# Input projection of the token mixer: float32 products become three single-pass products of split operands

## The reference, cut to what matters

```python
def token_mix(hx, hc, w_in, ...):
    def project(h):
        return jnp.split(h @ w_in, split_at, axis=-1)
    cq, cff, cfb, ci, cg, caq, cak, cav, cga, cgb = project(hc)
    ...
    xq, xff, xfb, xi, xg, xaq, xak, xav, xga, xgb = project(hx)
    xo, _, _ = hgrn_bidir(heads(xq, HG_HEADS), ..., cs_f, cs_b)
    ...
    y_x = merge(xo, xg, attend_blocks(xqa, keys, vals), xga, xgb)
...
x = x + g1 * y_x
x = x + g2 * expert_choice_moe(...)       # 16 experts, 12 MB of weights each
```

## Time and profile before

| | us |
|---|---|
| median of 3 runs | 1872.17 (1870.63 to 1873.43) |
| the profiled execution | 1873.85 |
| its span | 1872.1 |
| TensorE busy | 1716.0 (92%) |
| VectorE busy | 795.9 (43%) |
| ScalarE busy | 634.2 (34%) |
| GpSimd busy | 8.7 |
| first row of the projection to the end of its step 17 | 1083.6 to 1275.2 |
| expert stage | 1440 to 1872, 427 GB/s of loads |

### The profile page before, as it was taken

One profiled execution on the slowest core, in us unless ns is written; L12 is line 12 of the kernel. 1 busy time (PEld: TensorE's weight loads), 2 busy tenths in 40 slices (PEclk: granted clock), 3 DMA queues, 4 the chain that ended last, 5 costly groups with the idle time before them and its releaser, 6 DMA issues.

```text
span 1872.1 us, 30497 instructions
## 1 busy us (share of the span) xinstructions
PE 1716.0 (92%) x13205; PEld 1417.3 (76%) x13205; DVE 795.9 (43%) x1155; ACT 634.2 (34%) x899; POOL 8.7 (0%) x8
## 2 busy tenths in 40 slices
PE   8999999999999999999999999999999876765765
PEld 7999987899999999778999955877787442422422
DVE  6555697865566555224655522732512100000001
ACT  5444556644454444123444422415602010000101
POOL 0000010000000000000000000000000000000000
PEclk9999999999999999999999999999999997978987
DMA  9755456355545554552655532324566999999997
GB/s 291 241 166 193 158 181 201 118 198 181 183 154 188 192 180 140 164 173 94 199 182 192 164 113 68 113 90 158 216 258 247 427 425 427 427 426 426 426 427 327
DMA packets 189675, 427.45 MB, mean 228 GB/s; under 512 B 8004, under 2 KB 146678, under 8 KB 174485
## 3 DMA queue, kind: packets, MB, share of 16 engines
q1 hardware_dynamic: 189588, 426.19, 62.6%
HBM read 425.12 MB, written 1.05 MB: 228 GB/s over the span
## 4 chain that ended last, share of the span: by engine, by line
PE 74%; DMA 20%; DVE 3%; ACT 2%; issue 0%; another core or an unknown queue 0%; SPq 0%; DVEq 0%; ACTq 0%
PE banks L658 15%; PE banks L660 14%; PE banks L659 14%; DMA arena<-in_w_exp_down 5%; PE banks L1027 5%; PE banks L1003 3%; DMA ring<-in_w_exp_gate 3%; DMA xn<-in_w_exp_up 3%; DMA h<-in_w_exp_down 3%; DMA squares<-in_w_exp_gate 3%; DMA arena<-in_w_exp_up 2%; DMA ring<-in_w_exp_up 2%; PE banks L829 2%; PE banks L1300 1%; PE banks L781 1%; PE banks L1170 1%
## 5 line engine op out<-in xcount | busy, mean ns | idle before, releaser
L658 PE MATMUL banks<-x_split,w_split 128*128 128x256 f32 x1600 | 457.1, 286 | 9.5 <-DVE w_split L1873 4.0
L659 PE MATMUL banks<-x_split,w_split 128*128 128x256 f32 x1600 | 453.4, 283 | 0.0
L660 PE MATMUL banks<-x_split,w_split 128*128 128x256 f32 x1600 | 453.3, 283 | 0.0
L1873 DVE TENSOR_TENSOR w_split<-ring,w_split 128x1024 fp32r<-128x1024 f32 x288 | 346.5, 1224 | 237.7 <-ACT w_split L1396 237.3
L1396 ACT ACTIVATE w_split<-ring 128x1024 fp32r<-128x1024 f32 x287 | 295.2, 1051 | 190.5 <-PE banks L660 188.2
L658 PEld LDWEIGHTS banks<-x_split,w_split 128*128 128x128 f32 x1600 | 307.8, 192 | 13.3 <-issue 5.8
L659 PEld LDWEIGHTS banks<-x_split,w_split 128*128 128x128 f32 x1600 | 307.7, 192 | 0.3
L660 PEld LDWEIGHTS banks<-x_split,w_split 128*128 128x128 f32 x1600 | 307.7, 192 | 0.0
L658 PE MATMUL banks<-hid_split,w_split 128*128 128x256 f32 x704 | 199.6, 284 | 0.0
L659 PE MATMUL banks<-hid_split,w_split 128*128 128x256 f32 x704 | 199.2, 283 | 0.0
L660 PE MATMUL banks<-hid_split,w_split 128*128 128x256 f32 x704 | 199.2, 283 | 0.0
(11 more groups left out here) (387 smaller groups left out, 1945.8 us busy)
## 6 DMA issues: line engine op xcount, KB each, us to landing
ring<-in_ffn_w SPq DMA_DIRECT2D x131, 1024.0 KB, 5.3
arena<-in_w_exp_gate SPq DMA_DIRECT2D x13, 2048.0 KB, 45.9
ring<-in_w_mod SPq DMA_DIRECT2D x24, 1024.0 KB, 5.2
arena<-in_w_exp_down SPq DMA_DIRECT2D x12, 2048.0 KB, 45.0
arena<-in_w_exp_up SPq DMA_DIRECT2D x11, 2048.0 KB, 46.4
ring<-in_w_in SPq DMA_DIRECT2D x21, 1024.0 KB, 5.3
ring<-in_w_exp_down SPq DMA_DIRECT2D x9, 2048.0 KB, 44.3
ring<-in_w_exp_gate SPq DMA_DIRECT2D x7, 2048.0 KB, 45.9
```

The source lines that it names most:

```text
L658: mm(out_, hi, moving(0), start=start, stop=False, **kw)
L659: mm(out_, hi, moving(1), start=False, stop=False, **kw)
L660: return mm(out_, lo, moving(0), start=False, stop=stop, **kw)
L1873: ins = dve.tensor_tensor(half_part(n, o, 1), half_slot(n, o, columns), half_part(n, o, 0).bitcast(F32), ALU.subtract)
```

## The change

Steps 1 to 21 of the projection become three products of split operands, and step 0 stays as it is. ACT rounds the rows to `x_hi` (in ring slots 4 and 5) and DVE subtracts in place (`x_rest` is `xn`). For each piece ACT rounds both halves (`split_in`) into one of two buffers, the memory of the gates ga and gb (`w_gates`); the low part is the piece itself, subtracted in place in its ring slot (`w_rest`). DVE does both halves, except for pieces 8 to 15, whose second half GpSimd does. `split_in(s)` waits until the piece that had its buffer before has been multiplied, mostly s - 2, and the ring has only four slots from `mod_final` on. `ak` is multiplied once for both heads, and ACT writes the doubled halves with four copies; `av` is multiplied with the weights standing and then turned by four transposes. The last 1 MB loads of the mixer and the first expert tiles stand in another order. In `mla_a` the two halves of the last piece alternate for each k.

```diff
+FOUR_FROM = FIRST["mod_final"]
+PLACE = [n % SLOTS if n < FOUR_FROM else (n - FOUR_FROM) % 4 for n in range(FIRST["experts"])]
+PRIOR = [max([m for m in range(n) if PLACE[m] == PLACE[n]], default=None) for n in range(len(PLACE))]
+LOADS = [PLACE[:n + 1].count(PLACE[n]) for n in range(len(PLACE))]
+LAST_IN = [max(n for n in range(len(PLACE)) if PLACE[n] == p) for p in range(4)]
...
+        x_hi = nc.alloc_sbuf_tensor_at("x_hi", [P, KD, 2 * T], F32R, offset=ring_at + 4 * 4 * SLOT)
+        x_rest = nc.alloc_sbuf_tensor_at("x_rest", [P, KD, 2 * T], F32R, offset=xn_at)
+        w_rest = nc.alloc_sbuf_tensor_at("w_rest", [P, 4, KD, 256], F32R, offset=ring_at)
+        w_gates = split_tensor("w_gates", [P, 2, SLOT], gates_at)
+        w_roots = nc.alloc_sbuf_tensor_at("w_roots", [P, KD, P], F32R, offset=roots_at)
...
+        HI_BEFORE = {14: 12, 15: 12, 16: 14, 17: 15, 18: 16, 19: 17, 20: 18}
+        ON_POOL = list(range(8, 16))
+        LO_DVE = {(s, o): i + 1 for i, (s, o) in
+                  enumerate((s, o) for s in range(1, 21) for o in range(2) if o == 0 or s not in ON_POOL)}
...
+            branch_load(0)
             sp.wait_ge(sem("hg_normed"), 1)
             for i in (20, 8):
                 tile_load(i)
+            branch_load(1)
             sp.wait_ge(sem("att_ready"), 1)
             for i in (0, 1, 2, 3, 5):
                 tile_load(i)
-            w_out_load(2)
-            sp.wait_ge(slot_free, FIRST["branch"] + 1)
+            branch_load(2)
+            branch_load(3)
+            for i in (12, 13):
+                tile_load(i)
+            w_out_load(0)
             for i in (4, 6, 7):
                 tile_load(i)
+            w_out_load(1)
+            tile_load(9)
+            w_out_load(2)
             w_out_load(3)
-            sp.wait_ge(slot_free, FIRST["branch"] + 2)
-            tile_load(9)
-            for i in (17, 10):
-                wait_free(sp, N_EXPERTS + FIRST_IN_RING[i])
-                tile_load(i)
             sp.wait_ge(sem("merged_ready"), 2)
             for i in (14, 15):
                 tile_load(i)
-            for i in (11, 12, 13, 16):
-                wait_free(sp, N_EXPERTS + FIRST_IN_RING[i])
-                tile_load(i)
+            for p in sorted(range(4), key=lambda p: LAST_IN[p]):
+                sp.wait_ge(slot_free, LAST_IN[p] + 1)
+                tile_load((16, 17, 10, 11)[p])
...
-                for o in range(2):
-                    for k in range(KD):
-                        if j == 0 and o == 0 and k % 2 == 0:
-                            pe.wait_ge(sem("piece_normed"), NORM_PIECES["mla"] + k // 2 + 1)
-                        if j < 3:
+                if j < 3:
+                    for o in range(2):
+                        for k in range(KD):
+                            if j == 0 and o == 0 and k % 2 == 0:
+                                pe.wait_ge(sem("piece_normed"), NORM_PIECES["mla"] + k // 2 + 1)
                             last = mm(ps[:, j, o * T:o * T + T], slot(n)[:, k * 256 + o * P:k * 256 + o * P + P],
                                       x_in[:, k, :], start=(k == 0), stop=(k == KD - 1))
-                        else:
+                else:
+                    for k in range(KD):
+                        for o in range(2):
                             last = mm(ps[64 * o:64 * o + 64, j, 0:T], slot(n)[:, k * ROPE:k * ROPE + ROPE],
                                       x_in[:, k, :], start=(k == 0), stop=(k == KD - 1))
...
+                wait_rest(s, 0)
+                if name == "i":
+                    wait_rest(s, 1)
+                    lo = w_rest[:, PLACE[n], :, :]
+                    for t in range(4):
+                        for k in range(KD):
+                            tokens = slice(t * P, t * P + P)
+                            for part, (x_, w_) in enumerate(((x_hi, w_hi(s)), (x_hi, lo), (x_rest, w_hi(s)))):
+                                last = mm(ps[:, b + t // 2, (t % 2) * T:(t % 2) * T + T], x_[:, k, tokens], w_[:, k, :],
+                                          start=(k == 0 and part == 0), stop=(k == KD - 1 and part == 2))
+                    done(last)
+                    return
+                wide = name in ("ff", "fb", "ak", "av")
+                pe.wait_ge(sem("x_parts"), 6 if wide else 2 if step == 1 else 4)
+                rows = slice(0, 2 * T) if wide else slice(T, 2 * T)
+                for o in {"ak": (0,), "av": (1,)}.get(name, (0, 1)):
+                    if o == 1:
+                        wait_rest(s, 1)
+                    out_ = ps[:, b + (o if name in ("ff", "fb") else 0), :] if wide else ps[:, b, o * T:o * T + T]
+                    for k in range(KD):
+                        if step == 1 and o == 0 and k == 4:
+                            pe.wait_ge(sem("x_parts"), 4)
+                        hi, lo = w_hi_half(s, o)[:, k, :], w_lo_half(s, o)[:, k, :]
+                        mm(out_, hi, x_hi[:, k, rows], start=(k == 0), stop=False)
+                        mm(out_, hi, x_rest[:, k, rows], start=False, stop=False)
+                        last = mm(out_, lo, x_hi[:, k, rows], start=False, stop=(k == KD - 1))
...
+            for t in range(4):
+                last = pe.transpose(ps[:, 7, t * P:t * P + P], att_v[:, t, :], ident)
+            last.then_inc(sem("pe_mark"), 1)
...
+            def split_in(s):
+
+                n = w_in_slot(s)
+                if s >= 3:
+                    act.wait_ge(slot_free, w_in_slot(HI_BEFORE.get(s, s - 2)) + 1)
+                wait_full(act, n)
+                for o in range(2):
+                    fn(w_hi_half(s, o), w_in_half(s, o), ACT.Copy).then_inc(sem("w_hi_ready"), 1)
...
+            NEXT = {step: step + 2 for step in range(1, 12)} | {13: 14, 14: 15, 15: 16, 16: 17}
             for step in range(EARLY):
                 taken(step)
+                if step in NEXT:
+                    split_in(NEXT[step])
...
+            for s in ON_POOL:
+                pool.wait_ge(sem("w_hi_ready"), 2 * s)
+                pool.tensor_tensor(w_lo_half(s, 1), w_in_half(s, 1), w_hi_half(s, 1).bitcast(F32), ALU.subtract
+                                   ).then_inc(sem("w_rest_pool"), 1)
...
+            def rest_in(s):
+
+                for o in range(2):
+                    if (s, o) in LO_DVE:
+                        dve.wait_ge(sem("w_hi_ready"), 2 * s - 1 + o)
+                        dve.tensor_tensor(w_lo_half(s, o), w_in_half(s, o), w_hi_half(s, o).bitcast(F32), ALU.subtract
+                                          ).then_inc(sem("w_rest_ready"), 1)
...
+            REST = {0: 8, 1: 9, 2: 10, 3: 11, 4: 12, 5: 13, 7: 14, 8: 15}
             for r_ in range(ROUNDS):
+                if r_ in REST:
+                    rest_in(REST[r_])
```

More of the change, by code:

```diff
@@ L393, in wait_free @@
         def wait_free(sp, n, more=0):
-            if n >= SLOTS:
-                sp.wait_ge(slot_free, n - SLOTS + 1 + more)
+            if PRIOR[n] is not None:
+                sp.wait_ge(slot_free, PRIOR[n] + 1 + more)
         def wait_full(pe, n, more=0):
-            pe.wait_ge(slot_full[n % SLOTS], 16 * (n // SLOTS + 1) + more)
+            pe.wait_ge(slot_full[PLACE[n]], 16 * LOADS[n] + more)
         def wait_done(eng, n, more=0):
@@ L411, in slot @@
         def slot(n):
-            return ring[:, n % SLOTS, :]
+            return ring[:, PLACE[n], :]
         def half_slot(n, o, columns):
@@ L572, in _, with branch_load @@
                     mod_chunk(11)
[L573 to L576, removed]
+            def branch_load(j):
+                cols(FIRST["branch"] + j, (w_branch_a_2, w_branch_b_2)[j // 2][0], 512 * (j % 2), 512, 4)
             exp_tiles = [w[0].rearrange("e (j p k) c -> j e p (k c)", p=P, k=4)[j]
@@ L996, in project @@
                 b = 2 * (step % PAIRS) if step < EARLY else LATER_BANK[step - EARLY]
-                wait_full(pe, n)
                 if PAIRS <= step < EARLY:
                     pe.wait_ge(sem("proj_taken"), step - PAIRS + 1)
-                if name in ("ff", "fb"):
+                if step == 0:
+                    wait_full(pe, n)
                     for o in range(2):
                         for k in range(KD):
[L1003 to L1019, removed]
-                            last = mm(ps[:, b, t * P:t * P + P], xn[:, k, t * P:t * P + P],
-                                      slot(n)[:, k * 256 + P:k * 256 + 256], start=(k == 0), stop=(k == KD - 1))
-                else:
-                    for o in range(2):
-                        for k in range(KD):
-                            if step == 0 and o == 0 and k % 2 == 0:
+                            if o == 0 and k % 2 == 0:
                                 pe.wait_ge(sem("modulated"), SHIFTED["tokens"] + k // 2 + 1)
@@ L1036, in _ @@
                 if step == 0:
+                    pe.wait_ge(sem("mod_taken"), 4)
+                if step == 2:
                     pe.wait_ge(sem("squares_added"), 5)
@@ L1554, in _ @@
```

(27 more changed lines are left out.)

92 lines of the change are left out of this document (67 added, 25 removed).

## The result

The changed kernel takes 1846.4 us (median; 1845.5 to 1847.3) where the kernel before takes 1872.2: a ratio of 0.986, 95% interval 0.985 to 0.988, 25.8 us less. The forecast was 1842.6 with a range of 1830 to 1856.

What follows compares the result with a forecast made beforehand. TensorE was taken to bound the projection and DMA the expert stage. Gains of 38.1 + 2.3 - 0.7 + 2.7 = 42.4 us, less 12.8 lost in the rounds, left 29.6 off 1872.17: 1842.6 us, range 1830 to 1856.

Steps and rivals of the forecast that it cites:

- Bound and place of the gain: Before the experts: TensorE time gained ahead of 1435 moves the expert stream forward, except just ahead of two ACT/DVE places.
- The products: Projection up to the end of step 17: split products, 0.12 us narrow and 0.22 wide, save 38.1 us.
- near the record of the same width: Price of a split product of 512 columns, absent from the trace: taken as 0.22 us, bounds 0.215 and 0.240.
- The rounds: From step 8: DVE and GpSimd block each other on a shared port; 12.8 us lost, including 1 at the entry.
- the wait at the entry: When step 8 begins, DVE has no lead after the scans; 1 us of wait was counted.
- the branch of 14.8: In the rounds, DVE waits for GpSimd's port: 13.8 us plus 1 at the entry, weighted 0.75.
- The four transposes: Turning av behind step 17: 8 added records of 0.11 us, 0.9 less 0.2 idle, cost 0.7 us.
- Step 20: Between rotation and router: attention work waits only for it; steps 20 and 21 together gain 2.3 us.
- a clock under 1.0 in the projection: Granted TensorE clock in the projection: named as a sign against the whole forecast, with no size given.
- 18 and 19 give nothing: Steps ahead of waits for DVE's products ending at 1283.5 and 1316.0: shortening them gains nothing.
- mla_a: Half-array piece of the latent projection: alternating halves cut 6.3 us to 3.6, a gain of 2.7.
- The tail rivals: Slower GpSimd operations (3.5 us: 1849) or late expert tiles (four more: 1852); chance 0.17 together for 1847 to 1857.

Runs made afterwards that it cites:

- pool_left_out: The changed kernel without GpSimd's eight subtractions, TensorE taking the first half's low part for the second in pieces 8 to 15: 1835.98 us.
- warm: The changed kernel with eleven products of zeros in TensorE's idle time ahead of the attention's rotation (line 1162): 1844.70 us.
- pool_none: The changed kernel with VectorE making both halves of all low parts and GpSimd none: 1839.98 us, ratio 0.982.
- none_warm: The changed kernel with all low parts made by VectorE and eleven products of zeros ahead of line 1162: 1838.10 us, ratio 0.982.
- halves_alone: The kernel before with only the loop order of the latent projection's last matrix changed, so the halves alternate: 1870.04 us, ratio 0.9986.

## Why the prediction was right, and where its steps were off

**Bound and place of the gain: right.** TensorE's gain ahead of the experts reached the end: from the router on, both kernels take the same time to within 1.8 us, 1.15 of them step 21. SP's first reload of a buffer comes at 1407.2, and at 1435.4 before: 28.2 us earlier, nearly the whole of what the span lost.

**The products: one term too cheap.** Narrow steps took 5.74 to 5.84 us (forecast 5.76), steps 6 and 7 together 22.83 (23.04). The wide product was the open price, bounded by 0.215 and 0.240 and taken at 0.22; it measures 0.231 in steps 2 to 5 and 0.235 in ak and av. The step that failed is the choice "near the record of the same width". Half of that record is 0.215, and the split product lies 16 to 20 ns above it, where the one of 256 columns lies 12 ns above its half. So the extra grows with the columns, though less than in proportion; even the 12 ns once would have given 0.227, above the 0.22 that was taken. It cost 4 x 0.54 + 0.7 = 2.9 us.

**The rounds: the mechanism right, the sum right, its parts not.** From the end of step 7 (1160.4) to the last round's scores (1239.2) TensorE needed 78.8 us. Without any wait it is 65.2: 5.74 for step 8, and 59.4 for the eight distances as `pool_left_out` has them. So 13.6 were lost, where the sum had 12.8, weighted from 14.8 (VectorE always waits) and 6.7 (GpSimd does). All eight meetings went the first way. But the wait at the entry was 4.1 us and not 1: `pool_left_out` shows 2.0 of it as DVE's own list, and the rest is GpSimd's first operation, which fell on a scan, ahead of the rounds. Step 8 then ran 2.65 us longer, at a clock of 0.50 for part of it, and the sum had nothing for that. Against it, four distances were long by 0.6, 2.1, 2.1 and 2.0 us, 6.8 in all, where the sum had 13.8 for six rounds. The fifth distance was 7.4 us: no operation of GpSimd fell in it, which stood idle for 13.9 us, until 1219.6, waiting for ScalarE's next rounding. So 5.8 us too little and 7.0 us too much stood against each other in the branch of 14.8, and that the total came out within 0.8 of the weighted 12.8 is luck. The 2.65 and the 0.6 belong together: in `warm`, with the same wait of 3.96 us and the same list of VectorE, step 8 took 7.02 us and the next distance was 9.30, together 16.3, and 16.4 here. VectorE's list sets that time, not the clock. By the difference to `pool_left_out`, which lost 3.5 in the same stretch, GpSimd's half cost 10.1 us of these; 1.5 of the 3.5 are the lower clock in step 8 of that one execution, which there did cost time.

**Behind step 17: signs right but for one.** Steps 18 and 19 gave nothing, as forecast. The four transposes cost about 0.2 and not 0.7. Step 20 was to give 1.15 and gave -1.5: the clock, 2.7 us by the traces of the changed kernel and of `warm`. The prediction called a clock under 1.0 in the projection a sign against all of it and priced none. That sign came true in step 8, where it cost nothing, and at the rotation, where it did; the step that failed there is the sentence that "18 and 19 give nothing". A step that gives nothing because a wait follows makes the wait longer, and here the longer wait cost what step 20 gained and more.

**mla_a: right,** 2.6 us for 2.7.

**The tail rivals** did not occur: GpSimd's operation took 2.4 us, about twice its row of 512 columns, not 3.5; over the last 434 us the DMA share is 0.98 in both kernels, at 415 and 414 GB/s, so nothing points to a late tile.

From the forecast gain of 29.6 to the measured 25.8: -2.9 wide products, -0.8 rounds, -2.7 clock at the rotation, +0.5 transposes make 23.7. Some 2 us are left on the side of the gain: the scores of a round took 1.70 us and not 1.78 (0.7 in nine), and the last stretch ends 0.6 earlier than step 21 explains. What the rest is can't be told from the spread between executions.

## What to carry to other kernels

Before giving half of a job to GpSimd to relieve VectorE, compare two numbers: what VectorE needs for it (here 1.1 us) and how long GpSimd holds the memory for it (2.4 us, of which VectorE lost 2.1). Where VectorE's other operations read two inputs from SBUF, the help costs more than the work; an operation of GpSimd that only writes, or one beside VectorE work on the banks, was free. And where an edit shortens work ahead of a wait, price the longer idle time of TensorE as well, by the rows behind the wait at either clock. Products of zeros in the wait kept the clock up here; they must end before the chain needs TensorE. It matters only where TensorE, and not another engine, sets the time behind the wait.

## What the runs showed of the hardware

- The same idle time does not always lower the clock: behind 1.81 us of idle time at step 8 it stayed at 1.00 in `pool_none` and fell in `pool_left_out` and `none_warm` (to 0.57 and 0.51 in windows of the profile; step 8 took 1.5 us longer in each). Behind 2.66 and 3.96 us it fell in the changed kernel, and behind 2.66 in `pool_none` and `pool_left_out` too. In step 0 it fell in one execution of before and in `none_warm`, which made this step 1.6 us longer than in the others of nearly the same code (8.6 us, and 7.0 in `halves_alone`; 8.4, and 6.8 in `pool_none`).
- A lower clock costs nothing where TensorE isn't the bound. The 1.5 us were lost in `pool_left_out`, where TensorE set the pace, and not in `none_warm`. In the changed kernel step 8 took 8.39 us for 5.74, and the scores at 1190.5 took 3.34 for 1.95 behind an idle 1.84 (in the rows of TensorE above), while the chain ran through DVE, with issue times between its operations, from 1152.8 to 1209.2: what DVE's list takes sets the round either way.
- GpSimd waits for the VectorE operation under way, and sometimes for one more. Its third operation was issued at 1175.72 beside one of VectorE that had started at 1175.50; by its length (2.74 us for 2.40) it got in about 0.3 us later, and the next VectorE operation, at 1176.10, was held up. Its second was issued at 1165.59 beside one that had started at 1165.43; the next, at 1166.03, still ran in its usual 0.68 us, and the one at 1166.75 lost 2.1 us. What decides between the two, no run here shows.
